# A planner that knows ACT table loads, adaLN outputs in thirds, and one modulation block at another place

## The reference, cut to what matters

```python
mod = (silu(c) @ w_ada + b_ada).reshape(B, 9, 1024)
# sub-layer 0: FFN 1
hh = rms(x, g_norm[0]) * (1 + mo(1)) + mo(0)
x  = x + 0.5 * mo(2) * rms(swiglu(hh, w_ffn1_in, w_ffn1_out), g_norm[1])
# sub-layer 1: mixer (retention and gMLP side by side), w_in is 1024 x 7168
hh = rms(x, g_norm[2]) * (1 + mo(4)) + mo(3)
x  = x + mo(5) * rms(mixer(hh, w_in, w_ret_br, w_sg_br, w_out, ...), g_norm[3])
# sub-layer 2: FFN 2
hh = rms(x, g_norm[4]) * (1 + mo(7)) + mo(6)
x  = x + 0.5 * mo(8) * rms(swiglu(hh, w_ffn2_in, w_ffn2_out), g_norm[5])
```

## Time and profile before

| | us |
|---|---|
| median of 3 runs | 1795.77 |
| the runs | 1793.9, 1795.77, 1875.95 |
| the profiled execution | 1799.34 |
| its span, slowest core (core 0) | 1797.5 |
| spans of the other cores | 1769.9 to 1797.2 |
| PE busy in the span | 1395.0 (78%) |
| DVE busy | 623.7 (35%) |
| ACT busy | 632.2 (35%) |
| POOL busy | 165.7 (9%) |

### The profile page before, as it was taken

One profiled execution on the slowest core, in us unless ns is written; L12 is line 12 of the kernel. 1 busy time (PEld: TensorE's weight loads), 2 busy tenths in 40 slices (PEclk: granted clock), 3 DMA queues, 4 the chain that ended last, 5 costly groups with the idle time before them and its releaser, 6 DMA issues.

```text
span 1797.5 us, 20138 instructions; the slowest of 8 cores (1769.9 to 1797.5 us)
## 1 busy us (share of the span) xinstructions
PE 1395.0 (78%) x6796; PEld 647.9 (36%) x6796; DVE 623.7 (35%) x1115; ACT 632.2 (35%) x1096; POOL 165.7 (9%) x194
## 2 busy tenths in 40 slices
PE   3389879949957757795757885767896997997996
PEld 2334434424423333332333332332332443443443
DVE  2121142051147633425633426633315105205213
ACT  3221231131135456415556315566233114114111
POOL 1101101111100000010000010000010110110110
PEclk9599979959988978897968897978897997997997
DMA  8999999999994736398555497554597996998991
GB/s 204 177 155 151 156 153 153 159 153 153 152 154 72 114 62 97 48 123 111 94 73 75 52 122 107 94 94 48 72 133 100 128 158 125 127 155 152 117 129 47
DMA packets 201603, 213.38 MB, mean 119 GB/s; under 512 B 4512, under 2 KB 196000, under 8 KB 201504
## 3 DMA queue, kind: packets, MB, share of 16 engines
q0 software_dynamic: 194016, 188.89, 78.9%
q1 hardware_dynamic: 7488, 23.22, 3.7%
HBM read 388.38 MB, written 12.58 MB: 223 GB/s over the span
## 4 chain that ended last, share of the span: by engine, by line
PE 62%; DVE 11%; ACT 10%; DMA 9%; issue 8%; DVEq 0%; ACTq 0%; POOLq 0%; SPq 0%
PE ps L326 62%; DMA sb_W<-w_ffn_in 4%; ACT sb_UF L326 3%; ACT L326 3%; DVE sb_rstd_t L326 2%; DVE sb_tmpf L326 2%; DVE sb_UB L326 2%; DMA sb_W<-w_in 2%; ACT sb_UB L326 1%; DMA sb_W<-w_ada 1%; DMA sb_wsp_n<-w_sp 1%; DVE sb_stat L326 1%; DVE sb_rg L326 1%; ACT sb_sqb L326 1%; DVE sb_x_all L326 1%
## 5 line engine op out<-in xcount | busy, mean ns | idle before, releaser
L326 PE MATMUL ps<-sb_hTa,sb_W 128*128 128x512 bf16 x2688 | 641.2, 389 | 65.0 <-ACT sb_hTa L326 30.9
L326 PEld LDWEIGHTS ps<-sb_hTa,sb_W 128*128 128x128 bf16 x2688 | 266.4, 100 | 399.9 <-issue 102.3
L326 PE MATMUL ps<-sb_UB,sb_W 128*128 128x512 bf16 x1440 | 352.7, 384 | 4.2 <-DVE sb_UB L326 4.2
L326 PE MATMUL ps<-sb_W,sb_hTa 128*128 128x512 bf16 x864 | 237.2, 420 | 73.6 <-ACT sb_hTa L326 47.2
L326 ACT ACTIVATE sb_tmpf<-ps 128x512 f32<-128x512 f32 x180 | 104.5, 596 | 479.7 <-PE ps L326 350.0
L326 DVE TENSOR_TENSOR sb_UB<-sb_tmpf,ps 128x512 bf16<-128x512 f32 x132 | 88.7, 687 | 378.0 <-PE ps L326 349.0
L326 ACT ACTIVATE sb_UF<-ps 128x512 f32<-128x512 f32 (+2 forms) x196 | 110.5, 571 | 302.2 <-PE ps L326 280.9
L326 PEld LDWEIGHTS ps<-sb_UB,sb_W 128*128 128x128 bf16 x1440 | 141.7, 99 | 178.4 <-issue 14.6
L326 DVE RECIPROCAL sb_rstd_t<-sb_rstd_t 128x512 f32<-128x512 f32 x19 | 63.7, 3352 | 325.8 <-ACT sb_rstd_t L326 325.7
L326 PEld LDWEIGHTS ps<-sb_W,sb_hTa 128*128 128x128 bf16 x864 | 88.5, 106 | 194.6 <-issue 125.5
L326 ACT ACT_TABLE_LOAD x76 | 97.5, 1283 | 119.7 <-PE ps L326 54.7
(11 more groups left out here) (92 smaller groups left out, 966.0 us busy)
## 6 DMA issues: line engine op xcount, KB each, us to landing
sb_W<-w_ffn_in POOLq DMA_DIRECT2D x60, 1024.0 KB, 23.3
sb_W<-w_in POOLq DMA_DIRECT2D x45, 1024.0 KB, 17.9
sb_W<-w_ffn_out POOLq DMA_DIRECT2D x24, 1024.0 KB, 16.6
sb_W<-w_ada POOLq DMA_DIRECT2D x18, 1024.0 KB, 28.6
sb_W<-w_ffn_out POOLq DMA_DIRECT2D x12, 768.0 KB, 20.1
sb_UF<-x_in SPq DMA_DIRECT2D x12, 512.0 KB, 9.9
sb_W<-w_ffn_in POOLq DMA_DIRECT2D x12, 512.0 KB, 12.8
sb_W<-w_ret_br POOLq DMA_DIRECT2D x6, 1024.0 KB, 11.4
```

The costliest lines, as they stand in the source:

```text
L326: fn = lambda e: getattr(e, name)(*a, **kw)
```

## The change

It has three parts. The planner notes for silu, gelu, sigmoid, sqrt, exp and ln which table they need, adds 1300 ns to the start of an ACT candidate whose table differs from the one in use, and so prefers others that can start within that time. `mod_sub` adds the bias after every second block instead of once after six, so that a third of the vectors is one key of its own (`mod{L}_0`, `_1`, `_2`), and the derived `Apre` and `Gpost` follow their third. And `mod_sub(2)` stands behind `mixer_rest(0)`, instead of behind `ffn(0, 1)`; `mod_sub(1)` stays behind `ffn(0, 0)`.

```diff
@@ class Sched, reorder
+        cur_tbl = None
+        TBL = float(os.environ.get("K_TBL", "1300"))
...
-                    cand = (rt, i, e)
+                    if e == "act" and op.tbl is not None and op.tbl != cur_tbl:
+                        rt += TBL
                     if best is None or (rt, i) < (best[0], best[1]):
                         best = (rt, i, e)
                     if rt <= free[e]:
...
             op = rem[e].pop(i)
+            if e == "act" and op.tbl is not None:
+                cur_tbl = op.tbl
...
@@ R
+                if name == "activation":
+                    fn.tbl = {AF.Silu: "silu", AF.Gelu_apprx_tanh: "gelu", AF.Sigmoid: "sig", AF.Sqrt: "sqrt", AF.Exp: "exp", AF.Ln: "ln"}.get(kw.get("func"))
...
@@ mod_sub, in the loop over the six blocks
-            j0 = 24 * L
-            V(R("tensor_tensor", out=mod[:, j0:j0 + 24, :], in0=ps[:, PSM, 2 * j0:2 * j0 + 48].rearrange("p (j s) -> p j s", s=2),
-                in1=c(O_BADA + j0, 24).unsqueeze(2).to_broadcast([128, 24, 2]), op=ALU.add), (f"ps{PSM}", "small"), (f"mod{L}",))
...
+                if blk % 2 == 1:
+                    i_ = (blk - 6 * L) // 2
+                    j0 = 24 * L + 8 * i_
+                    V(R("tensor_tensor", out=mod[:, j0:j0 + 8, :], in0=ps[:, PSM, 2 * j0:2 * j0 + 16].rearrange("p (j s) -> p j s", s=2),
+                        in1=c(O_BADA + j0, 8).unsqueeze(2).to_broadcast([128, 8, 2]), op=ALU.add), (f"ps{PSM}", "small"), (f"mod{L}_{i_}",))
+                    coef = 1.0 if L == 1 else 0.5
+                    if i_ == 1:
+                        V(R("scalar_tensor_tensor", out=Apre[:, L], in0=modv[:, 3 * L + 1], scalar=1.0, in1=gnv[:, 2 * L].unsqueeze(2).to_broadcast([128, 8, 2]), op0=ALU.add, op1=ALU.mult),
+                          (f"mod{L}_1", "small"), (f"Apre{L}",))
+                    if i_ == 2:
+                        V(R("scalar_tensor_tensor", out=Gpost[:, L], in0=modv[:, 3 * L + 2], scalar=coef, in1=gnv[:, 2 * L + 1].unsqueeze(2).to_broadcast([128, 8, 2]), op0=ALU.mult, op1=ALU.mult),
+                          (f"mod{L}_2", "small"), (f"Gpost{L}",))
...
@@ norm_pre
-                  (f"tmpf{k % 3}", f"mod{L}"), (hp + str(k),))
+                  (f"tmpf{k % 3}", f"mod{L}_0"), (hp + str(k),))
...
+        MOD_AT = os.environ.get("K_MODAT", "f0,m0").split(",")
+        def maybe_mod(pt):
+            for L_, p_ in ((1, MOD_AT[0]), (2, MOD_AT[1])):
+                if p_ == pt:
+                    mod_sub(L_)
         for t in range(3):
             ffn(0, t)
-            if t < 2:
-                mod_sub(t + 1)
+            maybe_mod(f"f{t}")
         mixer_M12(1, full=False)
         for t in range(3):
             mixer_M12(t, full=True)
             mixer_rest(t)
+            maybe_mod(f"m{t}")
```

More of the change, by code:

```diff
@@ L32 @@
 class Op:
-    __slots__ = ("eng", "fn", "deps", "inc", "val", "sem", "waits", "is_dma", "tag", "idx", "cost", "fin", "bw")
+    __slots__ = ("eng", "fn", "deps", "inc", "val", "sem", "waits", "is_dma", "tag", "idx", "cost", "fin", "bw", "tbl")
 class Sched:
@@ L56, in add @@
         op.bw = getattr(fn, "bw", 0.0)
+        op.tbl = getattr(fn, "tbl", None)
         rd = tuple(k2 for k in rd for k2 in self.alias.get(k, (k,)))
```

## The result

The median of ten runs is 1806.14 us (1802.81 to 1876.58), against 1795.50 us for the kernel before in ten runs beside it: ratio 1.0059, 95% interval 1.0048 to 1.0070. The change costs some 10.6 us where a gain of 8 was forecast. One of these ten runs and two of the ten before took over 1870 us, the one after with four cores at a lower granted clock, and the ratio leaves these slow runs out. The profiled execution took 1802.81 us, its slowest cores (1 and 2) span 1801.0, the others 1784.6 to 1800.1.

A forecast was written before the change was run, and what follows sets the result against it. PE and weight supply were taken to run at the same pace, the bound changing by stage. Terms -17 + 12 + 0 - 3 = -8 took the profiled 1799.34 to 1791, 1788 on the median's scale; 8-in-10 range 1772 to 1808.

The forecast's parts named there:

- Part 1: FFN 1, mod_sub(2) leaves it: shorter gap between tiles 1 and 2 and a faster tile 2, -17 us.
- Part 2: Seam between mixer tiles 0 and 1, where mod_sub(2) enters: six loads ahead of the mixer's own cost +12 us.
- part 3: Bias addition split in each mod_sub: small DVE instructions and PE waits covered by block landings, 0 us, bounds 0 to +7.
- the -14.0: Gap between tiles 1 and 2 of FFN 1: falls from 37.2 to 23.2 us once mod_sub(2) is gone.
- tile 2 starts with full slots: FFN 1, tile 2: w_ffn_in loads take w_ada's queue places, so the tile takes 115.7 instead of 119.0 us, -3.3.
- The norm sums' reciprocal: Mixer's first seam: sums of squares wait behind w_ada's blocks, so the reciprocal comes at 841.5 instead of 836.53, +5 us.
- The first keys: Mixer's first seam: the key block lands at 849 against a start at 841.79, +7 us.
- The first gate: Mixer tile 1: first silu of the gate waits for a block landing at 883, so 885 instead of 875.34, +10 us.
- Part 4: Planner's table cost on ACT: up to six extra table loads saved, mainly in M3, -3 us, bounds -7.7 to +14.
- necessary ones, which gain nothing: The 70 table loads that dependences force, out of 76: they also pay the planner's price and gain nothing.
- slower: Rival: table cost puts M3's sqrt or silu behind other chunks' work, +29; total +24, 1820 us; chance 0.16.
- The move is a wash: Rival: mod_sub(2) costs at the mixer's seam what it cost in FFN 1; total +2, 1798 us; chance 0.19.

The follow-up runs named there:

- the move only: Against the kernel before: mod_sub(2) moved behind the mixer's tile 0, with no table cost and the bias added whole; ratio 1.0040.
- half the loads: The kernel with only mod_sub(2) moved, but three of its six w_ada blocks loaded, each read by the matmuls of two; ratio to the kernel before 0.9961.
- one load: mod_sub(2) moved into stage M3 of mixer tile 0, with one w_ada load in place of six, read by all 192 matmuls; ratio to the kernel before 0.9947.
- few matmuls: The kernel with only mod_sub(2) moved, all six loads, but 8 matmuls a block instead of 32; ratio to the kernel before 1.0040.
- a bank per third: The whole change, but each third of mod_sub has its own PSUM bank: ratio to the kernel before 0.9991; the same without table cost 1.0008.
- behind the norm: The kernel with only mod_sub(2) moved, but recorded behind norm_pre of tile 1 instead of ahead of it; ratio to the kernel before 1.0020.
- the spread pair: mod_sub(2) inside mixer tile 0's M3, mod_sub(1) in halves behind FFN 1's tiles 0 and 1; to the kernel before 0.9983, with table cost 1.0005.

## Why the prediction was wrong

The four terms, -17 + 12 + 0 - 3, all erred to the same side, by about 4, 3, 5 and 3 to 5 us, and no one of them alone turns the sign. The forecast first fails at the price of the move, parts 1 and 2 together: -5 was forecast, and the move only measured 1.0040, +7 us (+4 as a mean over the cores). Next comes part 3, the only term put at nothing.

**Part 1, -17 forecast, -13 found.** The gap fell by 13.65 (37.20 to 23.55), as the -14.0 said. The other term, "tile 2 starts with full slots and takes the 115.7 of FFN 2 instead of 119.0, -3.3", failed: the tile takes 118.95 with DMA at 0.89. The row of FFN 2 was misread. The stretch was cut at 1482.50 and has 525 matmuls where a tile has 534. Cut 2 us later it holds them all:

```profile
1366.80:1484.50 117.70, 117.65 (x534) 52.81 (x534) 18.85 (x28) 26.12 (x44) 14.76 (x17) 0.98 0.93 125
```

So the tile of FFN 2 takes 117.7 us, 1.3 less than in FFN 1 and not 3.3. The 52 matmuls of the row behind it are these 9, the 11 of a pure gap and 32 transposes of the output. And the 1.3 didn't come either, though supply was no longer the limit. The bounds of -10 to -18 held the truth; the reasoning from a supply limit didn't.

**Part 2, +12 forecast, +15 found.** The mechanism was right: six loads of 6.9 us ahead of the mixer's (half the loads, one load, few matmuls all agree). The size varies: m1 was 277.6, 272.1 and 271.2 in the kernels with the move alone and the stores in place, 275.6 with the table cost, and 267.2 and 270.1 with a bank per third. That is +7 to +17 on 260.3, and in the whole change +15.1. The norm sums' reciprocal came 8 us later behind M6 than before in the kernel after, where the forecast had +5. The first keys came 28 to 35 us behind M6 in the kernels with six loads, and 31 to 35 in the kernel after, instead of 23.4: +8 to +12 against +7. The first gate, forecast 10 to 16 later, came some 19 later with few matmuls and behind the norm (about 76 us behind M6 instead of 57), and 29 to 34 later in the whole change. That m1 pays only half of this shows that the gate, by which the +12 was chosen, isn't what decides; the size was right for a reason I can't show. Not foreseen was SP's store of states, which isn't moved, but at this seam now meets full DMA queues.

**Part 3, 0 forecast, +5 found.** The prediction saw the shared bank, and that "PE waits for DVE twice, and behind it the norm sums". It bounded that by the reciprocal, "if a planned reciprocal (3.35 us) comes first, +3.4 for each of two blocks". But a waiting PE waits for everything that the planner puts before the 0.17 us addition, and that was a reciprocal and 16 instructions, 218.49 to 232.06. Even with "bounds 0 to +7" the working took 0, for "a DVE that is idle while blocks land": DVE is not idle at that seam: `post_norm` runs there, and Part 1 of the same prediction names it as what is late next.

**Part 4, -3 forecast, a small loss found.** The table loads fell to 73, within the forecast's 70 to 76, and single mixer tiles did gain: m2 is 2.3 shorter after, m1 3.9 shorter in the spread pair. But m0 lost 2.1 in that pair, and the square roots at the FFN's seams, called "necessary ones, which gain nothing", lose 1.2 each, which the forecast had priced only for M3. One reading was off as well: the gelu whose table load is at 670.14 was called hidden behind DVE's variance. DVE's last instruction for it is this one,

```profile
670.69 0.16 DVE L326 SCALAR_TENSOR_TENSOR sb_stat<-sb_stat 128x4 f32<-128x4 f32 x1
```

and the load for the square root starts at 672.05, so only 0.7 of the 1.9 us were hidden. Alone the cost stands at 1.0008 with an interval that holds 1; beside spread blocks 1.0005 against 0.9983, a loss of 0.2%.

**Sum.** -13 + 15 + 5 and between 0 and +2 from the table cost: +7 to +9, against 10.6. The rival "slower" had its +24 in M3, from the table cost; the loss is real and lay elsewhere. "The move is a wash", -17 + 16 + 3 = +2, was the nearest: it had both true mechanisms, the full price of the seam, about right, and the split, too small, and took over the gain of part 1, which was 4 too large.

The load of 1283 ns that the Trainium skill gives, page "ScalarE: Activation LUTs", section "What ACT_TABLE_LOAD costs", is the mean in the traces of all kernels here. With the further drain of about 1380 ns that the section names, three loads fewer would be worth 8 us, as an estimate from its figures. The segments show no such gain, and no trace here shows the drain.

**Open.** The store's cost; whether the table cost does good or harm once the banks are apart; why m1 varies by some 10 us between kernels that move all six loads and, in the move only, from 270 to 287 between cores; and with it what a bank per third is worth at the mixer's seam.

## What to carry to other kernels

Splitting a result into finer keys (names by which the planner tracks who waits for what) saved nothing here, since the pieces shared a bank: it added a wait, whose price is not that of the small instruction that ends it but of all that its engine is given first. DMA that is spare over a stage isn't spare at a seam where slots are refilled in strict order; count how many blocks a seam holds (here four, at 6.9 us, in 23 us) and spread the rest over seams. A price on an unavoidable table load makes a greedy planner push other work before it, which cost 1.2 us at each seam of FFN 1; single mixer tiles gained 2 to 4 us in kernels that saved loads, and the sum was no gain.

## What the runs showed of the hardware

A table load wasn't run ahead of a wait: in the earlier trace rows it starts with the end of the instruction before, or, where the function behind it waits, only once that wait is over (656.12, after 1.40 us idle). A store of 512 KB from SP's queue landed late while POOL's loads filled the DMA engines: the first one behind the mixer's first seam took 6.4 to 8.2 us from issue to landing on the 8 cores of the kernel after, and 2.7 to 2.9 us in the kernel before. DVE waited 2.3 to 4.0 us for it on all 8 cores after and on none before; in the mixer's tile 0, about 610 us into the kernel, the kernel before has such waits too, 0.8 to 3.4 us. The weights' rate at full share was the same in both places: 7.0 us for 1 MB written in FFN 1 of the kernel before (landings from 355.6 to 397.4 us) and 6.9 us at the mixer's first seam of the kernel after (803.4 to 851.7).
